# Three groups of activations moved against the weight buffers, modulo 256 bytes

## The reference

```python
# first block
zl = hl @ w_in + b_in                       # 2048 x 13312; K and V also for 256 context tokens
y_na = neighbourhood_attention(...)         # 16 heads of 64
m = g_conv * (u @ w_conv_out) + g_sgu * (s @ w_sgu_out) + g_att * (y_na @ w_na_out)   # 1024 x 2048 each
x = x + mod[2] * (m @ w_o + b_o)            # 2048 x 2048
x = x + mod[5] * (square(relu(h @ w_ff1 + b_ff1)) @ w_ff2 + b_ff2)                    # 2048 x 8192 x 2048
# second block, 272 tokens
proj = hn @ attn_w_in                       # 2048 x 8192, then differential attention, 8 heads
h = h + rms_norm(o @ attn_w_out)            # 2048 x 2048
u, g = split(hn @ pool_w_in)                # 2048 x 4096; pooled, 4 groups of 512 x 512
h = h + rms_norm(mixed @ pool_w_out)        # 2048 x 2048
```

## Time and profile before

| | |
|---|---|
| median of 3 runs | 2854.0 us (lowest 2849.24) |
| the profiled execution's own time | 2853.54 us |
| its span, first to last instruction | 2851.8 us |
| TensorE: matmul busy | 2714.7 us, 95% |
| TensorE: weight load busy | 2553.3 us, 90% |
| VectorE busy | 1914.3 us, 67% |
| ScalarE busy | 1225.0 us, 43% |
| mean granted TensorE clock | 0.975 of full |

### The profile page before, as it was taken

One profiled execution on the slowest core, in us unless ns is written; L12 is line 12 of the kernel. 1 busy time (PEld: TensorE's weight loads), 2 busy tenths in 40 slices (PEclk: granted clock), 3 DMA queues, 4 the chain that ended last, 5 costly groups with the idle time before them and its releaser, 6 DMA issues.

```text
span 2851.8 us, 51278 instructions
## 1 busy us (share of the span) xinstructions
PE 2714.7 (95%) x21330; PEld 2553.3 (90%) x21330; DVE 1914.3 (67%) x2964; ACT 1225.0 (43%) x1801; POOL 219.7 (8%) x212
## 2 busy tenths in 40 slices
PE   5889999899999899999999999999999998979996
PEld 1279977699999899999999999999999997979996
DVE  5645667789999787875554555677656665477564
ACT  2122244544434544554443444564444444444453
POOL 4000011100003200100000000030000000220011
PEclk8899999999999999999999999999999999989998
DMA  7766643265878687865555555554434443535563
GB/s 252 256 206 236 222 148 116 88 219 160 267 245 256 202 276 258 270 230 195 180 190 183 186 184 187 179 194 155 155 133 158 148 154 110 185 108 177 189 194 110
DMA packets 163991, 539.01 MB, mean 189 GB/s; under 512 B 31024, under 2 KB 35120, under 8 KB 163632
## 3 DMA queue, kind: packets, MB, share of 16 engines
q1 hardware_dynamic: 163760, 535.73, 57.1%
HBM read 533.57 MB, written 2.10 MB: 188 GB/s over the span
## 4 chain that ended last, share of the span: by engine, by line
PE 80%; DVE 14%; issue 2%; DMA 2%; ACT 1%; SPq 1%; POOL 0%; POOLq 0%; ACTq 0%; DVEq 0%
PE ps L479 24%; PE ps L484 24%; PE ps L481 24%; DVE lo L1536 4%; PE ps L580 2%; DVE CV L1796 2%; PE ps L633 1%; PE ps L652 1%; DVE macc L1653 1%; DVE macc L1527 1%; DMA raw<-in_w_mod 1%; DVE macc L1524 1%; PE ps L641 1%; DMA raw<-in_w_in 1%; DVE row L2082 1%
## 5 line engine op out<-in xcount | busy, mean ns | idle before, releaser
L479 PE MATMUL ps<-AH,hi 128*128 128x256 f32 (+2 forms) x4480 | 1284.7, 287 | 13.5 <-DVE AL L2158 13.5
L484 PE MATMUL ps<-AH,lo 128*128 128x256 f32 (+2 forms) x4480 | 1271.8, 284 | 19.1 <-DVE lo L1536 19.1
L481 PE MATMUL ps<-AL,hi 128*128 128x256 f32 (+2 forms) x4480 | 1270.3, 284 | 0.0
L930 ACT ACTIVATE hi<-raw 128x1024 fp32r<-128x1024 f32 x808 | 850.9, 1058 | 929.3 <-PE ps L484 485.0
L1536 DVE TENSOR_TENSOR lo<-raw,hi 128x1024 fp32r<-128x1024 f32 x808 | 977.5, 1224 | 188.9 <-ACT hi L930 186.9
L479 PEld LDWEIGHTS ps<-AH,hi 128*128 128x128 f32 x4480 | 851.0, 190 | 45.5 <-issue 34.6
L484 PEld LDWEIGHTS ps<-AH,lo 128*128 128x128 f32 x4480 | 850.6, 190 | 22.0 <-DVE lo L1536 21.8
L481 PEld LDWEIGHTS ps<-AL,hi 128*128 128x128 f32 x4480 | 851.5, 190 | 0.8
L479 PE MATMUL ps<-YH,hi 128*128 128x256 f32 (+1 forms) x1536 | 434.9, 283 | 6.5 <-DVE YL L2093 6.5
L484 PE MATMUL ps<-YH,lo 128*128 128x256 f32 (+1 forms) x1536 | 434.1, 283 | 0.0
L481 PE MATMUL ps<-YL,hi 128*128 128x256 f32 (+1 forms) x1536 | 433.8, 282 | 0.0
(11 more groups left out here) (245 smaller groups left out, 2606.3 us busy)
## 6 DMA issues: line engine op xcount, KB each, us to landing
raw<-in_w_ff SPq DMA_DIRECT2D x256, 512.0 KB, 4.1
raw<-in_w_in SPq DMA_DIRECT2D x208, 512.0 KB, 4.4
raw<-in_w_mod SPq DMA_DIRECT2D x192, 512.0 KB, 4.5
raw<-in_w_ain SPq DMA_DIRECT2D x128, 512.0 KB, 3.5
raw<-in_w_pin SPq DMA_DIRECT2D x64, 512.0 KB, 3.5
raw<-in_w_o SPq DMA_DIRECT2D x32, 512.0 KB, 4.7
raw<-in_w_aout SPq DMA_DIRECT2D x32, 512.0 KB, 3.5
raw<-in_w_pout SPq DMA_DIRECT2D x32, 512.0 KB, 3.6
```

What stands on the lines that cost most here:

```text
L479: e.matmul(b.ap[:, o], hi[:, k, :], xh, start=start and k + i == 0, stop=False, skip_group_check=many)
L481: e.matmul(b.ap[:, o], hi[:, k, :], xl, start=False, stop=False, skip_group_check=many)
L484: mm = e.matmul(b.ap[:, o], los[j % NSPLIT][:, k, :], xh, start=False, stop=stop and k == KU - 1, skip_group_check=many)
L930: e.activation(his[u % NSPLIT][:, :, :], raws[i % NRAW][:, :].rearrange("p (k m) -> p k m", k=KU), ACT.Copy).then_inc(s_hi, 1)
```

## The change

Three pads of a size of their own take the place of one, and one small tensor goes. `pad0` (160 bytes) stands where the pad of 64 bytes was: all that lies behind it on the left, the weight buffers among it, moves up by 96. `onesf` (512 bytes) is gone; its one use, a 128 x 2 product ahead of everything, takes the matrix of 1/2048 and the exponential that reads it multiplies by 2048. `pad1` (128 bytes) lies in front of `G16`, behind which `BH` and `BL` lie. `pad2` (128 bytes) is at the right end and moves `CH`, `CL`, `YH`, `YL` (and what else is taken from the right) down by 128.

```diff
-        sb("pad", [128, 16])
+        sb("pad0", [128, 40])
         raws = [sb(f"raw{i}", [128, KU * 128]) for i in range(NRAW)]
...
-        onesf = sb("onesf", [128, 128])
         macc = [sb(f"macc{i}", [128, 512]) for i in range(2)]
+        sb("pad1", [128, 32])
         G16 = sb("G16", [128, 16 * T])
+        sb("pad2", [128, 32], F32, ctx, "right")
...
-            e.matmul(XB[:, 0:2], onesf[:, :], vt[:, LAMC:LAMC + 2], start=True, stop=True).then_inc(s_lamp, 1)
+            e.matmul(XB[:, 0:2], ones[2048][:, :], vt[:, LAMC:LAMC + 2], start=True, stop=True).then_inc(s_lamp, 1)
...
-            e.activation(vt[:, LAMC + 2:LAMC + 4], XB[:, 0:2], ACT.Exp).then_inc(s_lame, 1)
+            e.activation(vt[:, LAMC + 2:LAMC + 4], XB[:, 0:2], ACT.Exp, scale=2048.0).then_inc(s_lame, 1)
...
-            e.memset(onesf[:, :], 1.0)
```

## The result

The changed kernel is slower: median 2876.5 us of 4 runs, against 2851.6 of the kernel before in 4 runs, one of which, at 4522 us, the comparison leaves out. The ratio is 1.0093 (95% interval 1.0070 to 1.0116), about 25 us. I had forecast 14 us the other way.

The account below looks back on a forecast made before the run. TensorE's matmul step was taken to bound the kernel outside VectorE's stretch. From 2853.5 us, 14 us gained on packed operands and 0 elsewhere gave 2839.5, forecast 2840 us, chance 0.40; range 2790 to 2885.

Parts of the forecast that it names:

- What bounds the kernel: TensorE's matmul-to-matmul step sets the time nearly everywhere, except the wait up to 153 us and VectorE's stretch, 690 to 970 us.
- The step depends on where the operands lie, not on the clock or the other engines: Large products: activation and weight reads collide in SBUF; 256 columns take 113.3 or 117.7 ns at the same clock.
- The Trainium skill's rule: Rival for all matmuls: separate read ports make addresses irrelevant, so nothing changes, 2854 us; chance 0.09, shared with a stops-only rhythm.
- It is what a constant distance tends to: Packed `A`, `C`, `Y`: the clean 113.3 ns rhythm is likeliest, so two thirds of 22.5 us, 14 us, are gained.
- The bounds of the packed steps: Packed `A`, `C`, `Y`: from all at 113.3 ns, returning 22.5 us, to 123.3 ns each, losing 77 us.
- the two losses that I named: Packed products outside VectorE's stretch: all at 117.7 ns, 20 us, chance 0.15; or dearest collision every step, 77 us, chance 0.06.
- The small loss: Rival: 4600 packed matmuls outside VectorE's stretch settle at 117.7 ns, losing 4.3 ns each: 20 us, 2874 us; chance 0.15.
- The loss bounds: Packed operands lose up to 77 us, pool gate 4 of it; 272-column-group operands lose up to 36 us.
- The groups whose distance goes round count as zero: 258, 272 and last 256 columns, 8448 matmuls: a mean over four distances seems robust, so 0 of 48.7 us excess returns.
- 690 to 970 us show nothing, and `B` costs nothing: VectorE bounds these 280 us, hiding TensorE's changes; most of `B`'s 1152 matmuls run there, so 0 us.
- A stop throws the rhythm anew: Packed loops: a stop somewhere resets whether the two read streams collide, and the rhythm then stays for tens of microseconds.
- The dropped tensor: Dropping the memset of `onesf` at the start changes nothing; without the cover of waiting for data, well under 1 us.

Follow-up runs that it names:

- a constant 64: Weights' row groups put 576 instead of 512 bytes apart for `w_ff1` and second-block products, pads as before, four `lo`, against the kernel before: 2831.6 us, ratio 0.9940.

## Why the prediction was wrong

- **What bounds the kernel**: right. TensorE's busy time grew by 24.9 us and the span by 22.1.
- **The step depends on where the operands lie, not on the clock or the other engines**: shown. The Trainium skill's rule (SBUF — State Buffer, Who interferes with whom), by which TensorE never waits on anyone, doesn't describe this: `A` alone, moved by 96 bytes against the weights, costs 0.8%. The kernel with all addresses moved shows that the distance decides and not the address. That two reads of TensorE collide is still my reading; no run shows a collision as such.
- **"It is what a constant distance tends to", and so 14 us gained**: this step failed. I had one constant distance in the trace, 64, put it down as clean for over 60% of the packed time, and took the clean rhythm for a property of constant distances. The share was misread: of the 11520 packed matmuls outside the pool gate my own rows have 3072 in `w_ff2` and about 2000 elsewhere at 117.7, which leaves at most 56%, and counted unit by unit in the trace the share below 115 ns is 46%. And the tendency doesn't exist: of the eight distances 64 and 192 alone show 113.3 to 113.5 ns anywhere, 192 not in the two stretches compared, and the other six lie at 116.6 to 120.1. `A` at 160 runs at 120.0, so in place of a gain there came 5.5 us of loss in the last stretch, and 20.0 us from the first product to the last `B` (17.3 behind, after a start 2.7 ahead).
- **The bounds of the packed steps**: 113.3 to 123.3 ns did hold them, and the case that came out lies between the two losses that I named: 120, 118 and 118 ns, 22 us. The small loss, 2874 us, comes within 3 us of the measured 2876.5 by luck: it was priced with a mechanism that doesn't fit `A`, for `A` doesn't fall into 64's slow rhythm, it has a worse one of its own. The loss bounds also count the pool gate twice, once as packed (4 us) and once among the 272-column groups.
- **The groups whose distance goes round count as zero**: nearly right. 272 columns went from 126.2 to 125.2 ns in the stretches read, at most 4608 x 1.0 = 4.6 us gained; 258 columns moved by 0.2. The milestones show 0.6 us less between the last `B` and the last 272-column `Y`, after a loss in `w_o` and `w_ff2`.
- **690 to 970 us show nothing, and `B` costs nothing**: too small. The kernel with `B` alone moved costs 0.25%, not all of it where `B` runs. From the first to the last `B` the changed kernel loses 8.4 us, of which the part behind 980 us explains 4 (1236 matmuls at 119.1 ns against the mean of 113.4 and 117.8). `A` alone has 427.2 us there against 421.1 before, so most of the loss is `A`'s. VectorE is the bound of that stretch on the whole; that it isn't the bound of each unit is my reading, and I did not try what the rest hangs on.
- **A stop throws the rhythm anew**: incomplete. A burst of eight small matmuls without a stop changes it too, and the end of one product can hand its rhythm to the next: `pool_w_out` behind a `Y` at 32, and `w_ff2` behind `w_ff1`.
- **The dropped tensor**: nothing, as said.

Open: what the period of 256 and the order of the eight values come from, why 258 columns run slower with a constant 64 than going round, what throws 64 into the one or the other rhythm at the start, why a burst of small matmuls mostly changes it and sometimes not, and what the 0.25% of the kernel with `B` alone hangs on.

## What to carry to other kernels

Where matmuls of 256 columns each load new weights, the distance of the moving tensor from the weights modulo 256 can be worth 6% of the step; read it from the count in an even stretch, and try it with pads at one distance for all operands, one short run for each. Compare stretches that have the same step in several traces of unchanged distances, for one that takes either speed tells nothing. Don't judge a group by its own stretch alone: a good distance can be lost to the product in front of it, and gained from it. A tendency seen at one value of a parameter is no rule for the values that the trace has never had.

## What the runs showed of the hardware

- A 128-row float32r matmul of 256 columns with a weight load of its own starts every 113.3 ns at best at full clock. In `w_ff2` and `pool_w_out` it starts every 116.6 to 120.1 ns at seven of eight distances between the activations and the weights (multiples of 32, modulo 256; one execution each).
- At one distance the same product can have two lasting speeds: 113.3 and 117.7 ns at 64, 113.5 and 117.7 at 192, 117.3 and 118.7 at 96, 118.7 and 120.1 at 128. It can take the one or the other over from the product before it, and in two traces at 64 a burst of eight one-column matmuls changes it each time near 210, 240, 265, 1050, 1105 and 1160 us.
- The absolute addresses don't count where tried: everything moved by 96 bytes modulo 256 at distance 64, ratio 1.0003 (0.9990 to 1.0016).
